# Third mixer's gates as wide blocks: 512 columns per high weight, one PSUM bank per gate

## The reference

```python
y = jax.nn.sigmoid(gm + merge_gate_b[0]) * (hm @ w_up_m) \
    + jax.nn.sigmoid(gn + merge_gate_b[1]) * (on @ w_up_n)
x = x + y @ w_out
```

## Time and profile before

| | us |
|---|---|
| Median of 3 runs (lowest, highest) | 1437.62 (1437.16, 1437.67) |
| The profiled execution, its own time | 1437.53 |
| Its span in the trace | 1435.7 |
| TensorE busy | 1429.8 |
| VectorE busy | 984.9 |
| ScalarE busy | 801.9 |

### The profile page before, as it was taken

One profiled execution on the slowest core, in us unless ns is written; L12 is line 12 of the kernel. 1 busy time (PEld: TensorE's weight loads), 2 busy tenths in 40 slices (PEclk: granted clock), 3 DMA queues, 4 the chain that ended last, 5 costly groups with the idle time before them and its releaser, 6 DMA issues.

```text
span 1435.7 us, 20811 instructions
## 1 busy us (share of the span) xinstructions
PE 1429.8 (100%) x8064; PEld 1232.6 (86%) x8064; DVE 984.9 (69%) x1601; ACT 801.9 (56%) x1409; POOL 144.6 (10%) x212
## 2 busy tenths in 40 slices
PE   9999999999999999999999999999999999999999
PEld 7888888898888888888888898888888899888887
DVE  6656676777666566666676677665676977778776
ACT  6545556754555555455566746554557765465553
POOL 0100024000000001000050004000038300100000
PEclk9999999999999999999999999999999999999999
DMA  8655555354655547555564455556646335456551
GB/s 337 247 192 189 191 204 192 133 186 164 222 186 186 198 140 244 189 193 190 176 233 140 156 190 202 183 188 198 194 156 233 131 119 188 161 170 216 193 188 59
DMA packets 73681, 267.76 MB, mean 187 GB/s; under 512 B 8176, under 2 KB 8304, under 8 KB 73456
## 3 DMA queue, kind: packets, MB, share of 16 engines
q1 hardware_dynamic: 73296, 265.65, 55.0%
q10 hardware_dynamic: 288, 0.79, 0.1%
HBM read 265.36 MB, written 1.05 MB: 186 GB/s over the span
## 4 chain that ended last, share of the span: by engine, by line
PE 99%; DMA 0%; DVE 0%; POOL 0%; issue 0%; POOLq 0%
PE bank L559 30%; PE bank L566 15%; PE bank L513 9%; PE bank L514 9%; PE bank L515 8%; PE bank L580 4%; PE bank L585 4%; PE bank L581 4%; PE bank L543 3%; PE bank L550 3%; PE bank L544 3%; PE bank L533 1%; PE bank L748 1%; PE bank L759 1%; PE bank L774 1%; PE bank L806 1%
## 5 line engine op out<-in xcount | busy, mean ns | idle before, releaser
L1630 DVE TENSOR_TENSOR wlo<-raw,whi 128x1024 fp32r<-128x1024 f32 (+1 forms) x481 | 579.7, 1228 | 14.6 <-ACT whi L1097 14.6
L1097 ACT ACTIVATE whi<-raw 128x1024 fp32r<-128x1024 f32 (+1 forms) x481 | 490.0, 1048 | 5.5 <-DMA raw<-w_dram 2.9
L559 PE MATMUL bank<-hx,whi 128*128 128x512 f32 x1856 | 452.4, 392 | 0.0
L559 PEld LDWEIGHTS bank<-hx,whi 128*128 128x128 f32 x1856 | 343.7, 188 | 71.1 <-issue 3.0
L566 PEld LDWEIGHTS bank<-hx,wlo 128*128 128x128 f32 x1856 | 242.0, 191 | 11.7
L566 PE MATMUL bank<-hx,wlo 128*128 128x256 f32 x1856 | 245.5, 282 | 0.0
L513 PE MATMUL bank<-whi,hid 128*128 128x512 f32 x536 | 211.2, 394 | 0.2 <-issue 0.2
L514 PE MATMUL bank<-wlo,hid 128*128 128x512 f32 x536 | 209.9, 392 | 0.0
L515 PE MATMUL bank<-whi,hid 128*128 128x512 f32 x536 | 208.6, 389 | 0.0
L1726 DVE TENSOR_TENSOR sil<-sil,bank 128x256 f32<-128x256 f32 x80 | 33.6, 420 | 182.0 <-ACT sil L1186 182.0
L1186 ACT ACTIVATE sil<-bank 128x256 f32<-128x256 f32 x80 | 30.5, 382 | 211.4 <-PE bank L566 211.4
(11 more groups left out here) (256 smaller groups left out, 1536.1 us busy)
## 6 DMA issues: line engine op xcount, KB each, us to landing
raw<-w_dram SPq DMA_DIRECT2D x486, 512.0 KB, 3.5
gain<-g_dram SPq DMA_DIRECT2D x7, 512.0 KB, 4.2
arena<-c_dram SPq DMA_DIRECT2D x2, 768.0 KB, 6.0
cst<-c_dram SPq DMA_DIRECT2D x1, 1056.0 KB, 5.9
out_dram<-x SPq DMA_DIRECT2D x4, 256.0 KB, 2.0
par<-p_dram SPq DMA_DIRECT2D x1, 867.0 KB, 7.5
raw<-w_dram SPq DMA_DIRECT2D x2, 432.0 KB, 3.1
gain<-g_dram ACTq DMA_DIRECT2D x1, 512.0 KB, 4.8
```

Source lines behind the costliest of these rows:

```text
L559: e.matmul(b[:, :], hi_of(j)[:, k * P:k * P + P], hx[:, k * 2 * S:k * 2 * S + 2 * S], start=k == 0, stop=False, skip_group_check=True)
L1097: e.activation(hi_of(t), raw_of(t), ACT.Copy).then_inc(sem["w_hi"], 1)
L1630: e.tensor_tensor(lo_of(t), raw_of(t), hi_of(t).bitcast(F32), ALU.subtract).then_inc(sem["w_lo"], 1)
```

## The change

The third mixer's 16 gate tiles are done by `wide_block`, each in a bank of its own out of the same ring of two, and treated as in the other mixers: `gate_low` on ScalarE, `gate_add` on VectorE, `gate_of_sum` on ScalarE, one tile later. A bank is free when VectorE has added (`g_sum`). `gate_tanh` is gone; its waits on buffers stand in `gate_low`. On ScalarE and VectorE the new steps come after the two beats of the tile.

```diff
@@ banks
-                if tag == "M":
-                    claim(("Mg", f), "gate", 16 * m + 2 * f + 2)
-                else:
-                    for j in range(2):
-                        claim((f"{tag}g", f, j), "g_sum", 16 * m + 2 * f + j + 1)
+                for j in range(2):
+                    claim((f"{tag}g", f, j), "g_sum", 16 * m + 2 * f + j + 1)
@@ TensorE, mixer2
                 for f in range(KD):
-                    b = claim(("Mg", f))
                     for j in range(2):
-                        feat_block(T[f"Mg{j}{f}"], b[:, j * S:j * S + S], tick=tick)
+                        wide_block(T[f"Mg{j}{f}"], claim(("Mg", f, j)), tick)
@@ ScalarE
             def gate_low(m, f, j):
-                E.wait_ge("tile", DONE[f"L{m}g{j}{f}"])
-                E.wait_ge("qkt_t", 4 * m + 4)
+                tag = STAGES[(1, 4, 6)[m]]
+                E.wait_ge("tile", DONE[f"{tag}g{j}{f}"])
+                if m < 2:
+                    E.wait_ge("qkt_t", 4 * m + 4)
+                else:
+                    E.wait_ge("tile", DONE["Mvw13"])
+                    E.wait_ge("qkt_t", 8 + 2)
+                    if f >= 6:
+                        E.wait_ge("ml_s", 4)
...
                         ahead(T[f"Mg{j}{f}"])
                         tick()
                         tick()
-                    gate_tanh(f)
+                        gate_low(2, f, j)
+                        if f or j:
+                            gate_of_sum(2, 2 * f + j - 1)
+                gate_of_sum(2, 2 * KD - 1)
@@ VectorE
+            def gate_add(m, f, j):
+                g = gates[:, (2 * f + j) * S:(2 * f + j + 1) * S]
+                b = bank[K.BANK[f"{STAGES[(1, 4, 6)[m]]}g", f, j][0]]
+                E.wait_ge("g_low", 16 * m + 2 * f + j + 1)
+                e.tensor_tensor(g, g, b[:, 0:S], ALU.add).then_inc(sem["g_sum"], 1)
...
                         ahead(T[f"Mg{j}{f}"])
                         tick()
                         tick()
+                        gate_add(2, f, j)
```

More of the change, by code:

```diff
@@ L1283, in gate_low @@
             def gate_low(m, f, j):
-                E.wait_ge("tile", DONE[f"L{m}g{j}{f}"])
-                E.wait_ge("qkt_t", 4 * m + 4)
-                e.activation(gate_slot(f, j), bank[K.BANK[f"L{m}g", f, j][0]][:, S:2 * S], ACT.Copy).then_inc(sem["g_low"], 1)
+                tag = STAGES[(1, 4, 6)[m]]
[7 more added lines that the diff above has]
+                        E.wait_ge("ml_s", 4)
+                e.activation(gate_slot(f, j), bank[K.BANK[f"{tag}g", f, j][0]][:, S:2 * S], ACT.Copy).then_inc(sem["g_low"], 1)
             def gate_of_sum(m, n):
@@ L1293, in gate_of_sum @@
                 e.activation(gate_slot(f, j), gate_slot(f, j), ACT.Tanh, scale=0.5, bias=hb16[:, j * KD + f:j * KD + f + 1]).then_inc(sem["gate"], 1)
[L1295 to L1305, removed]
             def merge_tail(s, m):
@@ L1922, in mixer1 @@
                         tick()
-                        g = gates[:, (2 * f + j) * S:(2 * f + j + 1) * S]
-                        E.wait_ge("g_low", 16 * l + 2 * f + j + 1)
-                        e.tensor_tensor(g, g, bank[K.BANK[f"{tag}g", f, j][0]][:, 0:S], ALU.add).then_inc(sem["g_sum"], 1)
+                        gate_add(l, f, j)
                 merge_tail(s, l)
```

## The result

The changed kernel takes 1443.32 us (median of 5 runs, 1443.12 to 1443.86) against 1437.3 us (1437.11 to 1437.67): the ratio is 1.0042, 95% interval 1.0031 to 1.0053. It is 6.0 us slower. In the two profiled executions the span grew from 1435.7 to 1442.0 us, with TensorE's granted clock at 1.00 (2.4 GHz) in both; so a slower clock is not the cause.

A forecast was written before the change was run, and what follows sets the result against it. TensorE, busy 1429.8 of 1435.7 us, was taken to bound the kernel. Waits of 7.6 us, less 0.2 idle and 1.75 saved work, gave +5.7 to +5.8: 1437.53 + 5.8 = 1443.3 us, range 1438.0 to 1446.0.

The forecast's parts named there:

- Wait 1: Before tile 2 of the gates, TensorE waits 1.2 us for tile 0's bank, freed by VectorE's addition.
- Wait 2: In tile 2, TensorE waits 1.4 us for `ml_n` before `mlstm_scores`, where it had waited 0.2.
- Waits 3 and 4: TensorE waits before `mlstm_scores`, 0.5 us in tile 5 and 1.0 us in tile 8.
- Waits 5 and 6: Together 3.0 us over tiles 11 to 14, first at `turn_p`, then at the bank for tile 14.
- Wait 7: In tile 14 at `turn_p`, about 0.5 us, because it needs the sums behind another split.
- The saved work: On TensorE in the gates, 128 wide matmuls replace 128 narrow pairs: 1.75 us less.
- the pitch of a wide matmul: In the gates, 0.226 us per wide matmul against 0.240 us per narrow pair.
- The rule that I had left as a rival: Wide matmuls in the gates save only 2.5 ns a pair, an estimated 0.3 us for 128; (an estimated 1444.8); no chance of its own.
- That nothing waits: Rival: both gate banks come free within a tile, only the saved work counts, 1435.8 us; chance 0.08.
- That only the first period waits: Rival: the engines catch up in idle time after the gates' first period, 1438.2 us; chance 0.17.
- That every period costs as much as the first: Rival: 2.6 us of delay in each of five periods, 1448.8; chance 0.10 with other costs above 1446.
- The cover: Later weight splits (by up to 2 to 3 us) and raw loads in the gates stay hidden, costing nothing.

The follow-up runs named there:

- e3: The changed kernel with VectorE's next weight split put ahead of its addition, same work: 1440.29 us, ratio 1.002.
- e7: The changed kernel with VectorE's `mlstm_gate` moved from beat 69 to beat 71, nothing else: 1441.78 us, ratio 1.0029.
- e6: The reordered kernel e8 with each wide matmul replaced by two narrow ones into the halves of the same bank: 1438.78 us, ratio 1.0008.
- e8: The changed kernel with split first up to tile 12, copy between heads, `mlstm_gate` at beat 71, addition before double splits: 1437.41 us, ratio 0.9999.

## Why the prediction held

**Wait 1, the bank of tile 0.** Predicted 1.2 us. In the timeline the low part of tile 1 starts at 1141.35 and takes 0.95 start to start, so tile 2 was wanted at 1142.3 and came at 1143.37: 1.07. I had it wanted at 1142.0, with more work saved than was. The times of the copy and the addition were right within 0.05 us once the 0.17 is taken off by which this execution ran later here.

**Wait 2, `ml_n`.** Predicted 1.4 at line 1001. Measured 1.39, but in two pieces: first 0.6 us at `turn_p`, for VectorE's sums (the row at 1145.36), then 0.79 before line 1001. Both are work queued behind the addition; I had named only the second.

**Waits 3 and 4.** Predicted 0.5 and 1.0; measured 0.40 and 0.76 (from 1159.99 to 1160.71 and from 1172.35 to 1173.43, each less the 0.32 us of `turn_p`). e3 shows the mechanism: the split moved ahead of the addition takes both away.

**Waits 5 and 6.** Predicted 3.0 together, by the chain from line 2068 over GpSimd, line 2077, the addition, the exponentials and the bank of tile 14 at 1198.7. Measured 1.53 at `turn_p` in tile 11, released by ScalarE (the low part from 1187.73 on takes 0.96, then 1190.22), and 1.29 before tile 14 (1196.71, and 1198.95): 2.8. e7 shows that the second hangs on `mlstm_gate`; e3, where the first falls to 0.22 us, that it too is work behind the addition. From the start of tile 1 to that of tile 14 I forecast 60.2 us; it takes 60.1 (1138.83 to 1198.95).

**Wait 7.** Predicted 0.5, measured 0.60 (1200.94).

**The terms that were mis-sized.** The waits sum to 1.07 + 1.39 + 0.40 + 0.76 + 1.53 + 1.29 + 0.60 = 7.0 us, not 7.6. A wait costs a little more than the time until it ends: line 1001 takes 0.54 us to the next row after one (1160.71 to 1161.25) and 0.43 where nothing waits (in e3, 1158.88 to 1159.31), three times here and once before the change. That is 0.2 us, for which I had put nothing into the sum and up to 0.6 beside it. The saved work is what is left over: 7.0 and 0.2, less 0.2 that was there, less the 6.0 by which the stage grew, 1.0 us; the stages of e6 and e8 say the same. I had 1.75.

The step behind that term is the pitch of a wide matmul, and it is the one that failed. I took 0.226 us from 16 in a row, but in the gates a beat cuts each tile's eight into six and two. The six take 1140.22 - 1138.83 = 1.39 us, 0.232 each, where six pairs took 1.44. All of tile 1 took 3.55 us before (1138.64 to 1142.19); tile 4, which has the same small work and no wait, takes 3.47 (to 1158.60). So a tile gains 0.05 to 0.08 us and not 0.11. The cut is only part of it. In the first mixer an uncut eight can be seen, in the kernel before:

```profile
258.89 2.00 PE L559 MATMUL bank<-hx,whi 128*128 128x512 f32 x8
260.73 1.11 PE L566 MATMUL bank<-hx,wlo 128*128 128x256 f32 x8
```

These eight take 1.84 us, 0.230 each: the first five 0.232 each (258.89 to 260.05), the last three 0.227. They follow narrow matmuls, as each tile of the gates does; the sixteen of the earlier trace rows follow others of 512 columns. So the pace that I took is reached here only after some five wide matmuls, and a group of six has hardly any such. Why it starts slower no run shows.

The errors had opposite signs. The saved work was 0.75 us too large, which made the forecast too low. The waits with their ends were 0.4 us too dear (7.6 for 7.2), the sum of 5.65 was rounded up to 5.8, and the base to which it was added lay 0.2 us above the median (1437.53 for 1437.3), which made it too high by as much. That 1443.3 fell on the median is luck; that the mechanism and the places of the waits came out is not.

**The rule that I had left as a rival** (the Trainium skill, "TensorE: Matmul & The Clock Gate", Back-to-back issue gap, whose formula, given there for isolated matmuls, makes one wide one only 2.5 ns shorter than two narrow) does not agree with e6: at least 0.8 us for 128 pairs, 6 ns a pair, where it gives an estimated 0.3. But with about 1.0 us measured it was no farther off than my term of 1.75.

**The other rivals.** That nothing waits is refuted by the rows of TensorE; it needed another order of the queues. In e8, which has that order, the idle rows are down to 0.66 us, but its 1437.4 is not the 1435.8 of that rival, since those waits remain and the work saved is less. That only the first period waits is refuted by the rows from 1160 on. That every period costs as much as the first is too: 2.5 us in the first, 0.4 and 0.8 in the next two. **The cover** that I gave to splits and loads held: no idle row of TensorE in the gates is released by a weight split or a transfer, and the rest of the run takes 233.6 us as before.

What stays open: why the medians of e6 and e8 differ by 1.4 us where their stages, in one profiled execution each, differ by 0.8; and what a third bank would have been worth.

## What to carry to other kernels

Ask of an added step not how long it is but what stands behind it in its engine's queue: 6.7 us of additions on an engine busy for two thirds of the time cost 6.5 us, because VectorE stood 1.77 us before an addition (the rows at 1142.89 and 1198.47) and held up all that was queued after it. When buffers go from one per pair to one per item in the same ring, work out the hand-back of the slowest item (here exponentials, copy, addition), not the mean one. A saving of 0.1% is gone with the first wait; lay out the queues first, with the steps that others wait for ahead of those that only fill time, and change the work afterwards.

## What I had not expected of the hardware

A wide matmul saves less in short groups: 0.226 us each in a run of 16, 0.230 in an eight behind narrow ones, 0.232 in groups of six, and so 0.05 to 0.08 us a tile in place of 0.11. In the long runs of both shapes 256 columns more cost 0.106 us (0.226 less 0.120), which leaves an estimated 0.014 us per matmul whatever its width; that is all that merging two can save. And a TensorE that is given about 1.0 us more work while it is bound by others' queues made the run only 0.4 us longer, and the stage 0.3 (from 1134.14, where its tiles began, to 1208.34, against 73.9).
